# Weight-block sums of a seven-product FFN: from tensor instructions to accumulating transfers on GpSimd's queue, and the gated sums moved behind the third join

## What is computed

```python
def conv_ffn(hn, w_ffn_in, conv_w, conv_b, w_ffn_down):
    u, v = jnp.split(hn @ w_ffn_in, 2, axis=-1)          # 1024 -> 2 x 2816
    uc = conv_b + sum(pad(u)[:, t:t + L] * conv_w[t] for t in range(3))
    return (jax.nn.gelu(uc) * v).astype(dt) @ w_ffn_down  # 2816 -> 1024

h = h + token_mixer(rmsnorm(h, norm_mix), ...)
h = h + conv_ffn(rmsnorm(h, norm_ffn), ...)
return rmsnorm(h, norm_final)
```

## Time and profile before

| | |
|---|---|
| median of 3 runs | 1282.95 us (1281.03 to 1283.58) |
| the profiled execution | 1282.7 us, its span 1280.9 us |
| mean granted TensorE clock | 0.986 of full speed |
| busy, share of the span | PE 95%, DVE 68%, ACT 41%, POOL 15% |

### The profile page before, as it was taken

The page is one execution under the profiler, slowest core; times in us unless marked ns, Lnnn a source line. Parts: engine busy times, 40 slices in busy tenths (PEclk is TensorE's granted clock), DMA queues, the critical chain, the costliest instruction groups (busy, mean ns, idle before and its releaser), DMA issues.

```text
span 1280.9 us, 18435 instructions
## 1 busy us (share of the span) xinstructions
PE 1219.8 (95%) x6989; PEld 1108.8 (87%) x6989; DVE 875.3 (68%) x1189; ACT 528.7 (41%) x832; POOL 195.6 (15%) x137
## 2 busy tenths in 40 slices
PE   6999999999999999999999979899899899899977
PEld 5999999999999988888888869789789789789965
DVE  7494585486377372232233799988998998898987
ACT  5353353335245152122221456535535535535544
POOL 0000000000000000000000314324324333433340
PEclk9999999999999999999999999999899899899989
DMA  4311111101201011111123012112121121121302
GB/s 168 134 35 49 68 44 50 61 33 49 78 33 49 34 54 62 66 62 69 65 94 131 22 66 80 53 68 81 50 77 72 50 83 66 50 82 67 115 17 99
DMA packets 23185, 86.14 MB, mean 67 GB/s; under 512 B 2512, under 2 KB 2768, under 8 KB 23120
## 3 DMA queue, kind: packets, MB, share of 16 engines
q1 hardware_dynamic: 22544, 83.90, 17.7%
q10 hardware_dynamic: 576, 1.38, 0.3%
HBM read 82.12 MB, written 3.15 MB: 67 GB/s over the span
## 4 chain that ended last, share of the span: by engine, by line
PE 83%; DVE 10%; issue 2%; DVEq 2%; ACT 1%; DMA 1%; POOL 0%; SPq 0%; ACTq 0%; POOLq 0%
PE ps L1507 43%; PE ps L1750 19%; PE ps L1833 10%; PE ps L1604 3%; PE ps L1544 3%; DVE ring L1232 2%; PE ps L1597 1%; PE ps L1614 1%; PE ps L1532 1%; DVE cb L1315 1%; DVE cb L1296 1%; DVEq L1301 1%; DVE af L1251 1%; PE ps L1534 1%; DVE h L1219 1%
## 5 line engine op out<-in xcount | busy, mean ns | idle before, releaser
L1507 PE MATMUL ps<-hn,ring 128*128 128x256 f32 (+1 forms) x2544 | 462.6, 337 | 0.3 <-DVE hn L921 0.3
L1507 PEld LDWEIGHTS ps<-hn,ring 128*128 128x128 f32 x2544 | 388.3, 191 | 46.7 <-issue 0.7
L1750 PE MATMUL ps<-af,ring 128*128 128x384 f32 x1848 | 334.0, 340 | 33.0 <-DVE v L1288 21.0
L1750 PEld LDWEIGHTS ps<-af,ring 128*128 128x128 f32 x1848 | 325.8, 191 | 40.3 <-DVE v L1288 22.3
L1833 PE MATMUL ps<-ring,gf 128*128 128x512 f32 x693 | 161.0, 394 | 7.1 <-DVE gf L1331 6.8
L892 DVE TENSOR_TENSOR ring<-raw,ring 128x1024 fp32r<-128x1024 f32 x68 | 83.1, 1224 | 119.2 <-ACT ring L476 114.8
L1833 PEld LDWEIGHTS ps<-ring,gf 128*128 128x128 f32 x693 | 132.0, 191 | 35.1 <-issue 7.8
L1232 DVE TENSOR_TENSOR ring<-raw,ring 128x512 fp32r<-128x512 f32 x164 | 127.5, 810 | 13.5 <-ACT ring L713 13.3
L713 ACT ACTIVATE ring<-raw 128x512 fp32r<-128x512 f32 x164 | 96.6, 621 | 53.2 <-DMA raw<-in_pairs 42.0
L1467 POOL TENSOR_TENSOR sums<-raw 128x512 f32<-128x512 f32 x1 | 1.3, 1283 | 707.0 <-DMA raw<-in_pairs 707.0
L525 ACT ACTIVATE sig<-ps 128x768 f32<-128x768 f32 x36 | 29.2, 812 | 179.9 <-PE ps L1507 179.9
(11 more groups left out here) (171 smaller groups left out, 1297.8 us busy)
## 6 DMA issues: line engine op xcount, KB each, us to landing
raw<-in_units SPq DMA_DIRECT2D x68, 512.0 KB, 3.4
raw<-in_pairs SPq DMA_DIRECT2D x66, 512.0 KB, 3.5
strips<-in_strips SPq DMA_DIRECT2D x4, 896.0 KB, 4.6
x_in<-in_x_s SPq DMA_DIRECT2D x4, 512.0 KB, 5.4
h<-in_x_s SPq DMA_DIRECT2D x1, 2048.0 KB, 8.0
y_s<-hw SPq DMA_DIRECT2D x4, 512.0 KB, 3.0
x_in<-in_x_p SPq DMA_DIRECT2D x2, 512.0 KB, 7.4
h<-in_x_p SPq DMA_DIRECT2D x1, 1024.0 KB, 10.4
```

The lines of the kernel that those rows point to most:

```text
L1507: ins = pe.matmul(out, w if stationary_w else x, x if stationary_w else w, start=start and i == 0, stop=stop and i == 2)
L1750: ins = pe.matmul(ps[:, bank, 0:HALF], ring[:, p, a, k * P:(k + 1) * P], af[:, x, b, k, :], start=first and k == 0 and j == 0, stop=k == H ...
```

## The change

1. **Other sums.** The seven products use an equivalent scheme in which every weight combination is a sum: with blocks b11, b21 (u half) and b12, b22 (v half) they are S3 = b12+b22, S2 = b11+S3, S1 = b11+b12, A22 = S2+b21. The signs go to the combinations of tokens and gated blocks, to two joins and to the residual of S2 and S3, which subtract where they added. The number of instructions for these stays.
2. **Accumulating transfers.** From pair 1 on the weight sums are made by `sum_weights()`: four transfers a pair on POOL's queue, each of which adds a block of 256 KB to what stands in SBUF. Three read their block from HBM and one (S2) from SBUF. SP issues one transfer more for each pair, which puts b11 into the buffer `seconds`; the waits of the loads change with it. Pair 0 stays with POOL's instructions, with addition in place of subtraction.
3. **Gated sums.** The four sums of gated blocks leave `gate` and stand in `gate_sums`, behind `join_third` of the next pair. At a stage's end `conv` and `gate` of its last pair go into the down part, each behind a `down_sums`; in the last stage the low part of pair 20 goes ahead of `conv(21)`, and two low parts of pair 21 ahead of its sums.
4. **Beginning of the MLP.** S1 comes before S2 for pair 0, with the tokens' combinations in a matching order, and DVE's three differences for pair 1 are gone.

The core of the diff (left out: the same renaming in tables, semaphores, ACT's order at the beginning, and the signs in `combine_tokens` and the joins):

```diff
@@ -109,9 +109,8 @@
 
 for _lo, _hi, _qs in STAGES:
     SEQ += list(range(_lo, _hi)) + [down_pair(_q) for _q in _qs]
-    DIFFS += [(_i, _x) for _i in range(_lo, _hi) for _x in (S1, S2, S3, A22)]
-    DIFFS += [(down_pair(_q), _x) for _xs in ((S1, S2), (S3,), (A22,)) for _q in _qs for _x in _xs]
-DIFF = {_f: _n + 1 for _n, _f in enumerate(DIFFS)}
+    SUMMED += [(_i, _x) for _i in range(_lo, _hi) for _x in (S3, S2, S1, A22)]
+    SUMMED += [(down_pair(_q), _x) for _xs in ((S3, S2), (S1,), (A22,)) for _q in _qs for _x in _xs]
 LAST_Q = NQ - 1
 
...
@@ -316,28 +324,26 @@
 
         BANK_A, BANK_C = (0, 6), 7
 
-        def difference(eng, j, x):
-
-            r, second = raws[raw_of(j)], seconds[raw_of(j)]
-            b11, b21, b12, b22 = r[:, 0, 0:PIECE], r[:, 0, PIECE:UNIT], r[:, 1, 0:PIECE], r[:, 1, PIECE:UNIT]
-            if x == S1:
-                eng.wait_ge(pu_ld[raw_of(j)], 16 * loads_of(j))
-                eng.wait_ge(pv_ld[raw_of(j)], 16 * loads_of(j))
-                eng.wait_ge(flo, ORD[j, A11] + 1)
-                ins = eng.tensor_tensor(b11, b12, b11, ALU.subtract)
+        def sum_weights(pool, j, x):
+
+            b = raw_of(j)
+            r, second = raws[b], seconds[b]
+            u, v = pairs[j, 0], pairs[j, 1]
+            if x == S3:
+                pool.wait_ge(pv_ld[b], 16 * loads_of(j))
+                out, block = r[:, 1, 0:PIECE], v[:, PIECE:UNIT]
             elif x == S2:
-                eng.wait_ge(t_done, DIFF[j, S1])
-                if prior_of(j):
-                    eng.wait_ge(flo, ORD[prior_of(j), A22] + 1)
-                ins = eng.tensor_tensor(second, b22, b11, ALU.subtract)
-            elif x == S3:
-                eng.wait_ge(t_done, DIFF[j, S1])
-                ins = eng.tensor_tensor(b12, b22, b12, ALU.subtract)
+                pool.wait_ge(sec_ld[b], 16 * sums_of(j))
+                pool.wait_ge(t_sum[S3][b], 16 * sums_of(j))
+                out, block = second, r[:, 1, 0:PIECE]
+            elif x == S1:
+                pool.wait_ge(pu_ld[b], 16 * loads_of(j))
+                pool.wait_ge(flo, ORD[j, A11] + 1)
+                out, block = r[:, 0, 0:PIECE], v[:, 0:PIECE]
             else:
-                eng.wait_ge(t_done, DIFF[j, S2])
-                eng.wait_ge(flo, ORD[j, S2] + 1)
-                ins = eng.tensor_tensor(second, b21, second, ALU.subtract)
-            ins.then_inc(t_done, 1)
+                pool.wait_ge(flo, ORD[j, S2] + 1)
+                out, block = second, u[:, PIECE:UNIT]
+            pool.dma_start(out, block, accum_op=ALU.add).then_inc(t_sum[x][b], 16)
 
         def gate_place(q, x, b):
             return gf3[:, x, b, 0, :] if q == LAST_Q else gf[:, x, b, q % 2, :]
...
@@ -447,10 +453,14 @@
 
                     sp.wait_ge(fdone, ORD[NF - 1, A11] + 1)
                 else:
-                    sp.wait_ge(flo, ORD[prior, A22] + 1)
+                    sp.wait_ge(flo, max(ORD[prior, A12], ORD[prior, S1]) + 1)
                 sp.dma_start(raws[b][:, 0, :], pairs[j, 0]).then_inc(pu_ld[b], 16)
+                if j > 0:
+                    if prior is not None:
+                        sp.wait_ge(flo, ORD[prior, A22] + 1)
+                    sp.dma_start(seconds[b], pairs[j, 0][:, 0:PIECE]).then_inc(sec_ld[b], 16)
                 if prior is not None:
-                    sp.wait_ge(flo, ORD[prior, S4] + 1)
+                    sp.wait_ge(flo, max(ORD[prior, S3], ORD[prior, S4]) + 1)
                 sp.dma_start(raws[b][:, 1, :], pairs[j, 1]).then_inc(pv_ld[b], 16)
 
             sp.wait_ge(fdone, ORD[NF - 1, S4] + 1)
...
@@ -848,13 +860,15 @@
                 hi_upto(PLACE[hi - 1, A22] + 6)
                 centre(hi - 1)
                 hi_upto(PLACE[hi - 1, S4] + 6)
-                gelu(hi - 1)
                 if hi == NF:
                     gate_hi(NF - 2)
+                    gelu(hi - 1)
                     gate_hi(NF - 1)
                 for n, x in enumerate(DOWN[d]):
                     hi_upto(PLACE[down_pair(qs[-1]), x] + 6)
                     if n == 1 and hi < NF:
+                        gelu(hi - 1)
+                    if n == 2 and hi < NF:
                         gate_hi(hi - 1)
                     if hi == NF and n == 2:
                         act.wait_ge(fdone, ORD[NF - 1, S4] + 1)
...
@@ -1313,20 +1329,23 @@
                     dve.tensor_tensor(ge[:], cb[:], v2[:], ALU.mult).then_inc(g32_done, 1)
                     return
                 dve.tensor_tensor(cb[:], cb[:], v2[:], ALU.mult).then_inc(g32_done, 1)
+
+            def gate_sums(i):
+
+                q = i // 2
                 dve.tensor_tensor(GATE[S3], ge[:, 0:HALF], ge[:, HALF:T], ALU.subtract).then_inc(gs_done, 1)
                 dve.wait_ge(g32_done, i + 1)
                 dve.wait_ge(gs_done, 4 * q + 1)
-                dve.tensor_tensor(GATE[S2], GATE[A22], GATE[S3], ALU.subtract).then_inc(gs_done, 1)
-                dve.tensor_tensor(GATE[S1], ge[:, HALF:T], GATE[A22], ALU.add).then_inc(gs_done, 1)
-                if i == NF - 1:
-                    gate_lo(i - 1)
+                dve.tensor_tensor(GATE[S1], ge[:, HALF:T], GATE[A22], ALU.subtract).then_inc(gs_done, 1)
                 dve.wait_ge(gs_done, 4 * q + 2)
+                dve.tensor_tensor(GATE[S2], GATE[S1], ge[:, 0:HALF], ALU.subtract).then_inc(gs_done, 1)
+                dve.wait_ge(gs_done, 4 * q + 3)
                 dve.wait_ge(g_lo, gate_form(q, A11))
-                dve.tensor_tensor(GATE[S4], GATE[A12], GATE[S2], ALU.subtract).then_inc(gs_done, 1)
-
-            def gate_lo(i):
+                dve.tensor_tensor(GATE[S4], GATE[A12], GATE[S2], ALU.add).then_inc(gs_done, 1)
...
@@ -1369,10 +1388,7 @@
             dve.wait_ge(flo, ORD[0, S2] + 1)
             lo_form(5, S4)
             join_third(0)
-            difference(dve, 1, S1)
-            difference(dve, 1, S2)
             join_first(0)
-            difference(dve, 1, S3)
 
             for d, (lo, hi, qs) in enumerate(STAGES):
                 for i in range(lo, hi):
@@ -1393,23 +1409,30 @@
                     lo_upto(PLACE[i, S3] + 5)
                     if i > 0:
                         join_third(i)
+                    if i > lo and i % 2 == 0:
+                        gate_sums(i - 1)
                     if i > lo and i < NF - 1:
                         gate_lo(i - 1)
                 lo_upto(PLACE[hi - 1, A22] + 5)
                 lo_upto(PLACE[hi - 1, S4] + 5)
                 join_last(hi - 1)
-                conv(hi - 1)
                 if hi == NF:
+                    gate_lo(NF - 2)
+                    conv(hi - 1)
                     gate(NF - 1)
-                    gate_lo(NF - 1)
+                    gate_lo(NF - 1, GATES[1:3])
+                    gate_sums(NF - 1)
+                    gate_lo(NF - 1, GATES[3:])
                 for n, x in enumerate(DOWN[d]):
                     if hi < NF or n < 6:
                         lo_upto(PLACE[down_pair(qs[-1]), x] + 5)
                     if hi < NF:
                         down_sums(d, hi, qs, x, range(3))
                         if n == 0:
+                            conv(hi - 1)
+                        elif n == 1:
                             gate(hi - 1)
-                        elif n == 1:
+                        elif n == 2:
                             gate_lo(hi - 1)
                         continue
                     if n < 6:
...
-            pool.wait_ge(t_done, DIFF[1, S3])
-            for j, x in DIFFS[7:]:
-                difference(pool, j, x)
+            for j, x in SUMMED[4:]:
+                sum_weights(pool, j, x)
 
 
         @blk.tensor
```

More of the change, by code:

```diff
@@ L78, in taken @@
         if i == 0:
-            out += [(0, A11), (0, A12), (1, A11), (1, A12), (0, S2), (0, S1), (0, S3)]
+            out += [(0, A11), (0, A12), (1, A11), (1, A12), (0, S1), (0, S2), (0, S3)]
             continue
@@ L124, in loads_of, with sums_of @@
     return sum(raw_of(i) == raw_of(j) for i in SEQ[:SEQ.index(j) + 1])
+def sums_of(j):
+    return sum(i > 0 and raw_of(i) == raw_of(j) for i in SEQ[:SEQ.index(j) + 1])
 def prior_of(j):
@@ L283, in build @@
         pv_ld = [sem(f"pair_v_loaded{b}") for b in range(3)]
-        fhi, flo, fdone, t_done = sem("piece_hi"), sem("piece_lo"), sem("product_done"), sem("weights_combined")
+        fhi, flo, fdone, first_sum = sem("piece_hi"), sem("piece_lo"), sem("product_done"), sem("first_weights_combined")
+        sec_ld = [sem(f"second_loaded{b}") for b in range(3)]
+        t_sum = {x: [sem(f"weights{x}_summed{b}") for b in range(3)] for x in (S1, S2, S3, A22)}
         s_done, s_last, fyhi, fylo = sem("tokens_combined"), sem("last_tokens_combined"), sem("forms_hi"), sem("forms_lo")
@@ L375, in form_source @@
             a11, a12, a21, a22, second = token_blocks(t - 3)
-            return {S3: a11, S4: a12, S1: a21, A22: a22, S2: second}[x]
+            return {S2: a11, S4: a12, S3: a21, A22: a22, S1: second}[x]
         def form_place(o, x, b):
```

(50 more changed lines are left out.)

45 lines of the change are left out of this document (25 added, 20 removed).

## The result

The changed kernel takes 1296.36 us (median of 4 runs, 1293.82 to 1302.61) against 1283.0 us for the kernel before on the same chip (4 runs, 1281.03 to 1283.58). The ratio is 1.0114, with a 95% interval from 1.0077 to 1.0151: slower, by more than the 0.2% that counts, and above the predicted range of 1246 to 1290. The profiled execution took 1296.3 us, its span 1294.5 us.

The account below looks back on a forecast made before the run. PE was busy 95% of the span, so only its idle time and slow stretches could be won. 1282.7 - 39.7 of gains + 19.2 of loss gave 1262.2 us profiled, 1262.5 as median; range for 8 in 10: 1246 to 1290.

Parts of the forecast that it names:

- Parts 1 and 2: MLP: without POOL's instructions DVE runs undisturbed; gated sums behind the third join end four waits, 21.0 us, and 6.6 slow matmuls.
- Part 3: Last down part: pair 20's low part precedes conv(21), the 6.82 us wait goes, 2 us allowed; gain 7.3 us.
- part 5: Transfers slower than instructions: stage starts lose 3.9 us of gap and 0.9 of slow matmuls, four times; loss 19.2 us.
- D: The beginning of a down part, from which the chain to the next stage's start is timed; v half issued at D + 18.0.
- L: Time from POOL's issue of an adding transfer to its landing; unknown, taken as 4.1 us; stage-start gap 2L - 4.3.
- Within a stage the budget is wide: v half asked for two pairs ahead; S2 stands 16.8 us later against 3.5 + 2L, so no loss counted there.
- part 4: Smaller gains: 1.8 us from u halves loaded earlier, 3.0 of 3.6 at the MLP's beginning, 0 for S1 ahead of S2.
- earlier u halves: Waits of 1.56 and 0.26 us around the last down part go, as SP may load u halves after S1; 1.8 us.
- part 2: Gated sums behind the third join: four waits for join_third, 21.0 us, and 6.6 us of slow matmuls go.
- B: Rival, long transfers: slower at the stage starts, eating 39.7 us from L = 5.6; 1376 us at L = 8; chance 0.19.
- its term for POOL's queue: The long-transfers rival: POOL's queue, deciding from L = 6.1, adds 3.8 us for each of 17 pairs at L = 8, 65 us.

Follow-up runs that it names:

- e10: The changed kernel, with SP holding the loads of a stage's second pair until the first pair's S2 sum has landed; 1307.26 us, ratio 1.0171.
- e7: The changed kernel, with sums of pairs 5, 9, 13 and 17 (first of stages two to five) made by POOL's instructions; 1264.09 us, ratio 0.9847.
- e13: The changed kernel, with pair 1 and the first two pairs of stages two to five summed by POOL's instructions; 1254.01 us, ratio 0.9778.
- e8: The changed kernel, with adding transfers for the 11 down pairs alone and POOL's instructions for the input pairs; 1254.13 us, ratio 0.9769.
- e9: The changed kernel, all transfers kept, with gated sums, conv, gelu and gate back where they stood before; 1290.64 us, ratio 1.0047.
- e11: e8 with gated sums, conv, gelu and gate back where they stood in the kernel before; 1252.43 us, ratio 0.9758.
- e1: The kernel before, with only the new places of gated sums, conv, gelu and gate; POOL's instructions stay; 1277.29 us, ratio 0.9952.
- e6: The changed kernel with accum_op left out, so POOL's transfers write without adding and sums are left out; 1274.15 us, ratio 0.9924.

## Why the prediction was wrong

**What held.** Parts 1 and 2: DVE's low parts at 0.69 us (0.68 predicted), no wait for `join_third`, S4 at 2.2 us. That POOL's issuing of transfers doesn't slow DVE is as the Trainium skill has it (SBUF — State Buffer, Who interferes with whom: a DVE instruction with two SBUF inputs does not contend with a GpSimd instruction that only writes SBUF); this trace agrees with 688 ns. Part 3: -6.5 us against -7.3, with waits of 1.59 and 0.64 us where I allowed 2. The place of the new gap, by name and chain: at the first product of stages two to five, behind S2's piece and the residual.

**What failed first: the stage start in part 5, as a size.** It was 4 x (3.9 + 0.9) = 19.2 us and came to 24.1 us of waits and 8.2 us of slow matmuls (72 took 14.12 to 15.39 us, 12.6 undisturbed): 13.1 us more. Of the third stage's 1.9 us, the issue at D + 18.6 in place of 18.0 is 0.6, the v half's landing 0.95, and the two sums 8.7 against 8.3 us. That L = 4.1 fits this pair of sums is luck: S3's took 5.1 to 5.9 us in the four stages and S2's 3.3 in the third. I took 3.5 us for the v half from a kernel whose DMA engines were 18% busy, and used it for one where they are 65% busy; with the next pair's loads held back it was 3.9 us (e10).

**What failed most: "Within a stage the budget is wide".** I compared 16.8 us with 3.5 + 2L and left out that POOL's queue is in order, so that a late A22 sum of the first pair holds the S3 sum of the second, which then took 8.0 us and not 4.1. The waits behind it (1.5, 2.1, 0.5, 2.3, 0.2, and 0.3 and 2.7 near the end) sum to 9.6 us, and slower matmuls behind them to about 3.7. Of this nothing was in the sum. With the first pair by instructions the waits at the second fall to 1.1 to 1.9 us (e7), with the first two the stage runs through (e13). No run separates the order of the queue from the length of the sum.

**What failed third: the beginning in part 4.** Predicted -3.0 us, it came to +5.0 (-1.6 in the table, less the 6.6 us of the join that went): 1.5 us more of waits, with 4.56 us for `join_last` the longest, and 3.5 us of slower matmuls (276 took 50.94 us behind that wait, 48.2 undisturbed). Two causes can be told apart. With POOL's instructions for all input pairs (e8) this stretch takes 86.3 us, where I had forecast 82.0 and the changed kernel takes 90.0. So 4.3 of the 8.0 us of error have nothing to do with the transfers of input pairs. In e8 the waits there still sum to 8.4 us: the joins gave up 1.8, and 1.50 us for a third result and 0.63 us are new; and 12 matmuls behind a wait of 2.18 us took 3.59 us, where 2.4 is usual. Whether S1 ahead of S2, which I had priced at 0, does it or another part of the new beginning was not tested. The other 3.7 us are the transfers of pair 1 and later ones: I counted what the removed differences gave DVE, and not that pair 1 now depends on a chain of transfers. A22's sum was issued at 763.53 and its high part began at 769.78.

The 1.8 us that I gave to earlier u halves did not come either: the waits of 0.26 and 1.56 us are 0.34 and 2.69 us now, and 0.26 and 1.41 us in e13, where pair 21 has its early u half too. So the late u half was not what held them; what does is open.

Together: 13.1 + 13.3 - 0.4 (rounding) + 8.0 + 0.8 in the last part - 0.7 for the earlier start = 34.1 us, which is 1296.3 - 1262.2.

**One attribution was wrong though its number was right.** I put the 21.0 us down to part 2, above all to the order. e9 and e11 show that removing POOL's instructions for down pairs, which fell beside the gated sums, does it in the old order too, and e1 that the order without that only moves the gap. Had I priced the undisturbed sums in the earlier trace rows in the old order (four at 0.56 and not up to 1.47 us), I should have seen that the join would be in time without part 2.

**The rivals.** B had the side and the place, but its size only by accident: its rule 4 x (3L - 8.7 + 1.7), without its term for POOL's queue, gives 1296 near L = 6.8, and with that term near 6.3, but no sum of a stage's first pair took that long. The loss was that of shorter transfers in more places. The Trainium skill (DMA: Bandwidth & Descriptors, Anatomy of one DMA — SWDGE (gpsimd) path) gives, as an estimate from its fit, 2.6 us for 256 KB; the plain transfers of e6 took 2.7 to 3.4 us, the adding ones 3.4 to 5.2, so its fit is near for a plain copy and low for an addition.

**What stays open.** Why an adding transfer takes twice the engine time was not looked into. How much of 5.2 us is the addition itself and how much the company of other transfers is not separated: e6 bounds the two together at 1.8 us. The 4 us at the beginning moved from pair 1 to pair 2 as instructions took over pair 1, and went only with all input pairs by instructions (e8, e11); nothing between was tried.

## What to carry to other kernels

Before moving work from an engine to DMA queues, price the transfer at the load it makes, follow each queue in order past the first late item, and count the places with little time between load and use; there instructions stay (e7, e13), and transfers go where the use is far off (e8, e11). A gap that comes from one engine slowing another was cured here by taking the disturber away, and only moved by reordering the disturbed one (e11 against e1). Here 11 of 32 pairs by transfers give 1252 to 1254 us, 2.3 to 2.4% under the kernel before, 23 of 32 with the early pairs spared give 1254, and all of them 1.1% over it.

## What the runs showed of the hardware

An accumulating transfer of 256 KB used 1.8 times the packets of a plain one (18432 against 10240 for 33.56 MB) and twice the engine time (16.3% against 7.8% of the span). Issuing it held POOL 0.86 to 1.25 us in the third stage's timeline, against 0.54 us for a plain one in e6. SP's loads of 512 KB, beside it, landed after 4.8 us, beside plain transfers after 4.0, and alone after 3.5. Behind the wait of 6.31 us the granted clock was 0.50, TensorE's lower level of 1.2 GHz, from 1159.7 to 1163.7 us, 0.56 in the next 2 us and 1.00 after; behind the wait of 5.24 us in the kernel before it was 0.50 from 1016.3 to 1020.3 and 0.99 after. Shorter gaps were not free either: behind the 2.11 us gap the clock was 0.50 from 896.6 to 898.6, and behind the one of 2.29 us 0.57 from 1076.4 to 1080.4, which cost 1.7 and 1.5 us. A gap of 2.12 us in the kernel before, from which I took such gaps as free, was followed by a clock of 1.00. Over the span the granted clock was 0.978, against 0.996 in e8, whose gaps are short.
